# Heads of six tiles side by side with lagging low parts; norm sums and factors within a seventh tile

## What is computed

```python
def rms_norm(x, g):
    y = x * lax.rsqrt(jnp.mean(x * x, axis=-1, keepdims=True) + EPS)
    return y * g

xn = rms_norm(h, g_mix_pre);  z = xn @ w_in;  ...
h = h + rms_norm(mix, g_mix_post)
ff = jnp.square(jax.nn.relu(rms_norm(h, g_mlp_pre) @ w_up)) @ w_down
h = h + rms_norm(ff, g_mlp_post)
gate = jax.nn.sigmoid(rms_norm(h, g_ple_pre) @ w_ple_gate)
h = h + rms_norm((p @ w_ple_proj) * gate, g_ple_post)
# second block
z = rmsnorm(x, ln_mix_g) @ w_in_2;  ...;  x = x + merged @ w_out_2
a, u = split(rmsnorm(x, ln_ffn_g) @ w_ffn_in_2)
x = x + (silu(causal_dwconv(a, conv_w, conv_b)) * u) @ w_ffn_out_2
```

## Time and profile before

| | us |
|---|---|
| median of 3 executions (1488.62 to 1489.58) | 1488.74 |
| the profiled execution, its own time | 1483.36 |
| its span (first to last instruction) | 1481.6 |
| PE busy | 1454.1 (98%) |
| DVE busy | 798.1 (54%) |
| ACT busy | 560.2 (38%) |
| POOL busy | 267.8 (18%) |
| mean granted TensorE clock | 0.993 |

### The profile page before, as it was taken

One profiled execution on the slowest core, in us unless ns is written; L12 is line 12 of the kernel. 1 busy time (PEld: TensorE's weight loads), 2 busy tenths in 40 slices (PEclk: granted clock), 3 DMA queues, 4 the chain that ended last, 5 costly groups with the idle time before them and its releaser, 6 DMA issues.

```text
span 1481.6 us, 17750 instructions
## 1 busy us (share of the span) xinstructions
PE 1454.1 (98%) x6978; PEld 1187.9 (80%) x6978; DVE 798.1 (54%) x1155; ACT 560.2 (38%) x829; POOL 267.8 (18%) x180
## 2 busy tenths in 40 slices
PE   9999999999999999999999999999999999999998
PEld 7876768888888887767888888888887888888887
DVE  5687365433333346675767734634435665534554
ACT  5354434522324224443455546322224443323310
POOL 4255344300101012441033201300003000000000
PEclk9999999999999999999999999999999999999999
DMA  6221222332333332221211211323332233332331
GB/s 229 86 71 58 59 70 86 114 100 87 105 94 100 100 91 81 71 71 58 86 43 44 65 50 57 100 85 100 100 100 85 72 114 100 99 100 86 103 100 69
DMA packets 36131, 129.18 MB, mean 87 GB/s; under 512 B 4024, under 2 KB 4280, under 8 KB 36048
## 3 DMA queue, kind: packets, MB, share of 16 engines
q1 hardware_dynamic: 35760, 127.78, 27.8%
q10 hardware_dynamic: 288, 0.26, 0.1%
HBM read 125.91 MB, written 2.10 MB: 86 GB/s over the span
## 4 chain that ended last, share of the span: by engine, by line
PE 88%; DVE 5%; ACT 3%; issue 2%; POOL 2%; DMA 0%; ACTq 0%; DVEq 0%; POOLq 0%
PE P L1082 26%; PE P L1084 26%; PE P L1083 26%; PE P L1341 1%; POOL AC L2353 1%; PE P L1227 1%; DVE P L1895 1%; POOL H L2362 1%; DVE WST L2108 1%; PE P L1123 1%; PE P L1207 1%; PE P L1178 1%; PE P L1303 1%; POOL DD L2353 1%; PE P L1189 0%
## 5 line engine op out<-in xcount | busy, mean ns | idle before, releaser
L1082 PE MATMUL P<-AH,WH 128*128 128x512 f32 x1104 | 443.1, 401 | 10.0 <-issue 4.4
L1084 PE MATMUL P<-AH,WL 128*128 128x512 f32 x1104 | 432.2, 391 | 0.0
L1083 PE MATMUL P<-AL,WH 128*128 128x512 f32 x1104 | 431.9, 391 | 0.0
L1421 ACT ACTIVATE WH<-WR 128x1024 fp32r<-128x1024 f32 x232 | 243.9, 1051 | 339.3 <-PE P L1084 319.4
L1741 DVE TENSOR_TENSOR WL<-WR,WH 128x1024 fp32r<-128x1024 f32 x215 | 278.2, 1295 | 149.5 <-ACT WH L1421 148.9
L1082 PEld LDWEIGHTS P<-AH,WH 128*128 128x128 f32 x1104 | 208.6, 189 | 61.7 <-issue 13.1
L1084 PEld LDWEIGHTS P<-AH,WL 128*128 128x128 f32 x1104 | 208.3, 189 | 44.2
L1083 PEld LDWEIGHTS P<-AL,WH 128*128 128x128 f32 x1104 | 208.6, 189 | 41.9 <-issue 0.7
L1082 PE MATMUL P<-FH,WH 128*128 128x512 f32 x432 | 168.0, 389 | 0.0
L1083 PE MATMUL P<-FL,WH 128*128 128x512 f32 x432 | 168.0, 389 | 0.0
L1084 PE MATMUL P<-FH,WL 128*128 128x512 f32 x432 | 168.0, 389 | 0.0
(11 more groups left out here) (323 smaller groups left out, 1876.5 us busy)
## 6 DMA issues: line engine op xcount, KB each, us to landing
WR<-in_ws SPq DMA_DIRECT2D x232, 512.0 KB, 3.6
out<-Y SPq DMA_DIRECT2D x8, 256.0 KB, 2.0
H<-in_xT SPq DMA_DIRECT2D x3, 512.0 KB, 8.6
C<-in_const SPq DMA_DIRECT2D x1, 946.5 KB, 11.5
H<-in_xT SPq DMA_DIRECT2D x2, 256.0 KB, 4.2
PR<-in_pT SPq DMA_DIRECT2D x1, 512.0 KB, 4.8
WR<-in_ws SPq DMA_DIRECT2D x1, 384.0 KB, 4.7
WR<-in_ws ACTq DMA_DIRECT2D x1, 128.0 KB, 3.7
```

What stands on the lines that cost most here:

```text
L1082: e.matmul(P, wh, xh, start=start, stop=False)
L1083: e.matmul(P, wh, xl, start=False, stop=False)
L1084: ins = e.matmul(P, wl, xh, start=False, stop=stop)
L1421: e.activation(m.WH[:, c % NW, :], m.WR[:, c % NRAW, :], ACT.Copy).then_inc(*at.up("w_hi", "w_hi", c))
```

## The change

- A head has six tiles side by side (all four ring banks, 6 and 7) in every case, then a seventh, `last`, in bank 5, given by a step function `mid(last, j)`: a whole tile (`wide`), or in head 4 the narrow tile of gk (`narrow`, one step per slice now).
- Of the six, slice j runs WH·xh and WL·xh of each tile (`mm_hi`), and then WH·xl of slice j - 1 of each tile (`mm_lo`). The conversions (`ahead`) are named at `mm_hi` for chunks 0 to 2 and at `mm_lo` from chunk 3 on.
- `sums` stands at step 2 of the seventh tile, `spread` at step 6, both in bank 4; `rbc` after the tile.
- The stages' tile lists are moved up by one accordingly: glu(0), up(6), the seventh gate tile, gk, ffn_a(3) are seventh tiles. In the gate stage ple_gated(6) and its square stand before ple_gate(7).
- In mix2 (the last product before head 5) `x_hi`, `x_lo` and `square` of slices 0 to 5 of norm 5 are named within the loop; in head 5 only slices 6 and 7 remain.
- The number of blocks stays 1864.

```diff
+    def narrow(self, name, c0, n, kind):
+        ids = []
+        def step(t, j):
+            if j == 0:
+                ids.append(self.weight(tuple((0, n * q, name, 128 * q, 128, c0, n) for q in range(8))))
+            self.say("mm_narrow", t, ids[0], kind, n, j)
+        return step
+    def wide(self, spec, kind):
+        return lambda t, j: self.block(t, spec[j], (kind, j), j == 0, j == 7)
     def tokens(self, name, c0, nb, kind):
...
             self.say("square", s, 0, 0)
-        else:
+        elif s != "5":
             make(0)
             make(1)
             rest(0)
-        rest(1)
-        make(2)
-        got = [self.ring() for _ in range(3)] + [self.bank(b) for b in (6, 7)[:len(specs) - 4]]
+        if s != "5":
+            rest(1)
+            make(2)
+        got = [self.ring() for _ in range(4)] + [self.bank(6), self.bank(7)]
+        behind = []
+        def low(j):
+            for t, i in zip(got, behind):
+                if i // CH >= 3:
+                    self.ahead(i)
+                self.say("mm_lo", t, i, (x, j), j == 7)
         for j in range(8):
-            if j == 7:
-                self.sums(s, 0)
-            for m, t in enumerate(got):
-                self.block(t, specs[m][j], (x, j), j == 0, j == 7)
+            ids = []
+            for t, spec in zip(got, specs):
+                i = len(self.plan)
+                if i // CH < 3:
+                    self.ahead(i)
+                self.plan.append(spec[j])
+                ids.append(i)
+                self.say("mm_hi", t, i, (x, j), j == 0)
+            if j:
+                low(j - 1)
+            behind = ids
+            if s == "5":
+                if j < 2:
+                    make(j + 6)
+                    rest(j + 6)
+                continue
             if j < 5:
                 make(j + 3)
             if j < 6:
                 rest(j + 2)
-        b = self.spread(s)
-        out = got + [self.tile(specs[len(got)], [(x, j) for j in range(8)])]
+        low(7)
+        last = self.bank(5)
+        for j in range(8):
+            if j == SUMS:
+                self.sums(s, 0)
+            if j == SUMS + 4:
+                b = self.bank(4)
+                self.say("spread", s, b)
+            mid(last, j)
         self.say("rbc", s, b)
-        return out
+        return got + [last]
 
...
         for t in got:
             self.close(t)
         self.onpool = True
-        spec = tuple((0, 4 * j, "w_in", 128 * j, 128, 1280, 4) for j in range(8))
+        step = self.narrow("w_in", 1280, 4, "A1")
         t = self.ring()
-        self.say("mm_narrow", t, self.weight(spec), "A1", 4)
+        for j in range(8):
+            step(t, j)
         self.say("forget_in", t)
         self.close(t)
         self.beside(self.forget())
         for j in range(2):
-            t = self.tile(fm(128 * j), A)
+            t = self.tile(fm(128 * j), A) if j else out[6]
             self.say("glu", j, t)
             self.close(t)
...
-        out = self.head("2", ready, [fu(f) for f in range(6)])
+        out = self.head("2", ready, [fu(f) for f in range(6)], self.wide(fu(6), "A2"))
         self.say("ple_in")
-        for f in range(6):
+        for f in range(7):
             up(f, out[f])
-        for f in range(6, 8):
-            up(f, self.tile(fu(f), A))
+        up(7, self.tile(fu(7), A))
 
...
-        out = self.head("3", ready, [fg(m) for m in range(5)])
+        out = self.head("3", ready, [fg(m) for m in range(6)], self.wide(fg(6), "A3"))
         for m in range(8):
-            t = out[m] if m < 5 else self.tile(fg(m), G)
+            t = out[m] if m < 7 else self.tile(fg(m), G)
+            if m == 7:
+                self.say("ple_gated", 6)
+                self.say("square", "p3", 6, 1)
             self.say("ple_gate", m, t)
             self.close(t)
             if 0 < m < 7:
                 self.say("ple_gated", m - 1)
                 self.say("square", "p3", m - 1, 1)
-        for m in (6, 7):
-            self.say("ple_gated", m)
-            self.say("square", "p3", m, 1)
+        self.say("ple_gated", 7)
+        self.say("square", "p3", 7, 1)
         return self.post("p3", 1)
 
     def mixer2(self, ready):
...
-        out = self.head("4", ready, [fq(j) for j in range(4)] + [fm(at("ka")), fm(at("va"))])
+        out = self.head("4", ready, [fq(j) for j in range(4)] + [fm(at("ka")), fm(at("va"))],
+                        self.narrow(name, at("gk"), 16, "A4"))
         for j in range(5):
             self.say("qk2", j, out[j])
             self.close(out[j])
-        spec = tuple((0, 16 * j, name, 128 * j, 128, at("gk"), 16) for j in range(8))
-        t = self.ring()
-        self.say("mm_narrow", t, self.weight(spec), "A4", 16)
-        self.say("gk_low", t)
-        self.close(t)
         self.say("va_in", out[5])
         self.close(out[5])
+        self.say("gk_low", out[6])
         self.ya = self.yb = 0
...
             t = self.tile([block("w_out_2", 128 * q, 128 * m) for q in range(8)], [("M2", q) for q in range(8)])
             self.say("mix2", m, t)
             self.close(t)
+            if 0 < m < 7:
+                self.say("x_hi", "5", m - 1)
+                self.say("x_lo", "5", m - 1)
+                self.say("square", "5", m - 1, 0)
         return lambda m: None
...
-        out = self.head("5", ready, [fa(0), fa(1), fu(0), fu(1), fa(2), fu(2)])
+        out = self.head("5", ready, [fa(0), fa(1), fu(0), fu(1), fa(2), fu(2)], self.wide(fa(3), "A5"))
...
         first(2, out[4])
         second(2, out[5])
+        first(3, out[6])
+        second(3, self.tile(fu(3), A))
...
-        pairs(range(3, 8))
+        pairs(range(4, 8))
...
+    def mm_hi(t, i, x, start):
+        c, o = i // CH, (i % CH) * 128
+        P, xh = m.bank[t.bank][:], m.x(*x)[0]
+        part = int(o >= FIRST)
+        w.wait_ge(*(at("w_hi", c) if c else at("w_hi0", part)))
+        w.wait_ge(*at("x_hi", *x))
+        if start:
+            free(t)
+        e.matmul(P, m.WH[:, c % NW, o:o + 128], xh, start=start, stop=False)
+        w.wait_ge(*(at("w_lo", c) if c else at("w_lo0", part)))
+        e.matmul(P, m.WL[:, c % NW, o:o + 128], xh, start=False, stop=False)
+    def mm_lo(t, i, x, stop):
+        c, wh, wl, ends = weights(i)
+        w.wait_ge(*at("x_lo", *x))
+        ins = e.matmul(m.bank[t.bank][:], wh, m.x(*x)[1], start=False, stop=stop)
+        if stop:
+            ins.then_inc(*at.up("full", "full", t.id))
+            if ends:
+                at.also(("full", t.id), "w_used", c)
+        elif ends:
+            ins.then_inc(*at.up("w_used", "w_used", c))
```

More of the change, by code:

```diff
@@ L23 @@
 NBLK = 1864
+SUMS = 2
 NCHUNK = (NBLK + CH - 1) // CH
@@ L292, in spread, with head @@
         return t
-    def head(self, s, ready, specs):
+    def head(self, s, ready, specs, mid):
         x = "A" + s
```

32 lines of the change are left out of this document (17 added, 15 removed).

## The result

The changed kernel takes 1496.38 us (median of seven executions, 1493.28 to 1501.43), the kernel before 1488.74 (seven, 1488.09 to 1491.35): a ratio of 1.0057, interval 1.004 to 1.0073. It is slower by 7.6 us, where 7.5 was forecast. Comparing the two spans therefore exaggerates, and one reading has to come first: the clock.

A forecast was written before the change was run, and what follows sets the result against it. TensorE was taken to bound the kernel, busy 1454.1 of 1481.6 us. The terms gave +5.3 and clock slumps +2.2, total +7.5: 1496.2 us for the median, 0.5% slower; own range 1492 to 1500, full range 1486 to 1502.5.

The forecast's parts named there:

- Part 1: Head starts, needing only x(0)'s high part: heads 2 and 4 win 1.8 us, head 3 0.8, head 5 1.65; head 1 loses 1.1.
- Part 2: Sums and factors within the seventh tile: the waits of 0.66 and 3.28 us before the sums of heads 2 and 3 go.
- Part 3: Evictions after the seventh tile, all ring banks full: head 1 +2.0 us, head 2 0, heads 3 and 5 +0.7 each, head 4 +0.4.
- Part 4: Weight conversions queued behind seven evictions come late: stalls of +2.7 us after head 2 and +4.8 after head 5.
- has 5.5: After head 2's late conversion, the next chunk follows 3.8 us later and has 5.5 us; after head 5 no recurrence either.
- Part 5: Gate tiles of head 3: p3's sums 15.6 us after the seventh tile, some 9 us idle, only -1.5 of 7 won.
- Part 6: Forget gate before the first attention scores: a wait of about 2 us, half absorbed, so +1.0.
- the bound: Forget gate: bounds of 0 and 4 us, as glu(0) and five taps of 0.75 may come in between.
- Clock: Clock slumps behind the new conversion stalls: 1.7 us for head 5 and 0.5 for head 2, together +2.2.
- every stall is paid in full: Rival: slumps of 1.7 us at head 1, forget and head 2, forget wait not absorbed: +13, 1502; chance 0.17.
- Late conversions don't arise: Rival: conversions after heads 2 and 5 reach their queues in time, no stalls or slumps there: 1485 to 1486.5; chance 0.16.
- Gains and losses cancel: Rival: half the conversion stalls, no slump, head 4 at its full gain: +2, 1490.7; chance 0.15.

The follow-up runs named there:

- e3: The changed kernel with the sums at step 0 of the seventh tile instead of 2, factors likewise earlier: span x clock 1473.2 us, 6.0 below the changed kernel.
- e9: The changed kernel with sums and spread at steps 0 and 4, and tiles of up(7), ffn_u(3) and ffn_a(4) named early: median 1.002 of before.
- e1: The changed kernel with the tile of ffn_u(3) named directly behind the first eviction after head 5: span x clock 0.4 us lower than the changed kernel.
- 33 executions: The kernel before, unchanged, run beside the first experiments: median 1486.8 us, mean clock loss 12.9, span x clock 1472.4.
- e4: The kernel before with only norm 5's operands and squares for slices 0 to 5 made inside mix2: ratio 0.999 to before.
- e7: The changed kernel with head 3 and its gate tiles as in the kernel before: span x clock 0.9 us lower than the changed kernel.
- e8: The kernel before with lagging low parts and late sums in heads 2 to 5, five tiles (four in head 3), early norm 5 operands: 1479.24 us, ratio 0.9951.
- e11: The kernel before with late sums in heads 2 to 5 and early norm 5 operands, five tiles (four in head 3), no lag: span x clock 1470.6 us.
- e10: The kernel before with only lagging low parts in heads 2 to 5, sums where they were: 1499.3 us.
- e2: The changed kernel with up(7)'s tile named behind the first eviction after head 2: span x clock 3.0 us lower, clock loss 18.4 us.

## Why the prediction was right

*Starts of heads (Part 1).* Head 2 gained 1.84 (forecast 1.8), head 3 0.83 (0.8), head 5 1.65 (1.65). Head 4's row shrank by 1.25 only, but the gain of 1.8 is there: the first product used to come 1.90 us after the end of AH (644.53) and now comes 0.05 after it (655.56). The idle row starts at the end of the filler matmuls in front, and before, at a reduced clock, four of these took 2.52 us where they now take 1.88, so they hid part of the wait. Chunk 1 in head 1: the tokens come 7.72 later, 5.46 of it the extra tile and 1.16 the wait in front of them, which leaves 1.10 (forecast 1.1; the start of the program alone scatters by some 0.3 between executions).

*Sums within the seventh tile (Part 2).* No wait at either place. The step was right but not looked at from the other side: that the sums stood two steps later than they had to was worth 6.0 us (e3), the largest single term, and the forecast carried it inside Parts 3 to 5 without naming it.

*Evictions (Part 3).* Tokens 1.16 + 0.40 for 1.4 + 0.6; behind head 3 0.31 for 0.7, behind head 4 0.28 for 0.4, behind head 5 0.40 for 0.7. All were somewhat too large.

*Late conversions (Part 4).* The two chains came out as computed: R to conversion 17.44 us (forecast 17.45), copy to end of split 22.55 (22.7), waits 2.50 (2.7) and 4.52 (4.8). e3 and e9 shorten the chains and the waits follow. Only the confidence that the next chunk "has 5.5" us in hand belongs to mlp1; behind head 5 it has none (e1).

*Gates (Part 5).* The sums of p3 stand 15.7 us after the seventh tile's end (629.55), forecast 15.6. The wait in front is 7.11, not 9: between the last gate tile and the sums stand six filler matmuls that the sum left out:

```profile
635.43 2.74 PE L1238 MATMUL P<-C 128*128 128x512 f32 x6
```

They fill time and change nothing, so the elapsed time was right: head 3's start and gates together -1.2, forecast -1.5.

The rows also show who stretches whom beside GpSimd's adds of AC. The weight split took 1.97 us at 640.56, against the 2.03 of the earlier trace rows. The gates' TB steps, with one input in PSUM, kept 0.69; the Y steps, with both inputs in SBUF, grew from 0.69 to 1.06 and, the last one, to 1.25, and five adds of GpSimd took 8.19 (1.64 each, 1.29 alone). That is the pairing that the Trainium skill names (SBUF — State Buffer, "Who interferes with whom"). What it costs is, in the rows, about what GpSimd's instruction still has to run. Two places, of the gates and of the forget chain below:

```profile
643.87 1.26 POOL L2431 TENSOR_TENSOR AC<-AC,SQ 128x512 f32<-128x512 f32 x1 [2.42 <-ACT SQ L1521]
644.43 1.25 DVE L2089 TENSOR_TENSOR Y<-PJ,TB 128x512 f32<-128x512 f32 x1 [0.70 <-ACT TB L1631]
...
73.80 2.40 POOL L2421 TENSOR_TENSOR WL<-WR,WH 128x1024 fp32r<-128x1024 f32 x1 [7.28 <-ACT WH L1499]
73.91 2.83 DVE L1912 SCALAR_TENSOR_TENSOR FX<-FX 4x512 f32<-4x512 f32 x1
```

The add had 0.70 us left and the Y step took 0.56 more than its 0.69; GpSimd's split had 2.29 left and the FX step took 2.15 more than its 0.68. So the 0.8 of the earlier trace rows was right for this split, but it is no bound: a step that begins just behind GpSimd's can wait for nearly the whole of it.

*Forget gate (Part 6).* Mis-sized. The wait is 3.73, forecast about 2. VectorE's timeline:

```profile
68.39 0.67 DVE L1957 TENSOR_TENSOR UP<-P,SG 128x512 f32<-128x512 f32 x1
...
70.87 3.13 DVE L1973 SCALAR_TENSOR_TENSOR P<-UP,PM,P 128x512 f32<-128x512 f32 x4
78.02 0.42 DVE L1917 TENSOR_SCALAR FX<-FX 4x512 f32<-4x512 f32 x1
```

glu(0)'s product and five taps, 4.5 us, now stand between the forget steps; the prediction named them as what might come in between, but left them to the bound. They lengthen the chain by less than they take, from 8.94 us (59.34 to 68.28) to 10.66 (67.78 to 78.44), because VectorE used to be idle for 2.64 of these us. A smaller part of the miss is the transfer: from the last forget step to the first scores were 2.58 us, where some 2 was assumed. (An FX step stretched beside a GpSimd split, 2.83 here, was there before with 2.44.) Part of the wait is absorbed as argued: from the first scores to p1's sums the changed trace is 1.57 us shorter net of the clock, VectorE's 1.07 having gone. Net of both, forget costs about 2.2 us and not 1.

*Clock.* Forecast +2.2; it is +3.8 against the 33 executions and +0.8 against the seven. The argument (a slump behind 4.8 us of idle, none or a third of one behind 2.5) fits the profiled execution in these two places and misses the others:

```profile
81.00:85.00 4.00, 3.98 (x11) 3.23 (x12) 3.23 (x8) 1.82 (x2) 0.00 (x0) 0.50 0.30 114
...
644.00:648.00 4.00, 2.72 (x13) 2.75 (x14) 1.25 (x1) 1.03 (x2) 1.14 (x1) 0.50 0.29 115
...
1188.90:1192.90 4.00, 3.98 (x11) 3.19 (x12) 3.04 (x4) 1.58 (x2) 0.00 (x0) 0.57 0.43 131
```

(stretch, us, busy time of PE, PEld, DVE, ACT and POOL, granted clock, DMA share, GB/s). The falls behind the 3.73 and the 7.11 were not in the sum, though Part 5 had forecast 9 us of idle there, and three more (at 164, 708 and 928 us) have no wait over 0.6 us in front.

*The sum.* The parts were added up in elapsed time, and head 3's -1.5 counts the slumps behind 2.13 and 3.28 us as gone, 3.4 us of clock loss in the windows of before. So the 5.3 is no forecast of the rest, and the 2.2 is not the whole clock: taken apart, the forecast was about +8.7 and -1.2, and the means over the executions gave +6.8 and +3.8. In the two profiled executions, net of the clock, by the stretches above:

```
place                          forecast   measured, net of the clock
head 1 with the forget gate      +4.1       +4.6
head 2                           +0.2       +0.1
head 3 with its gates            -1.5       +0.9   (-1.2 elapsed)
head 4                           -1.4       -1.3
head 5                           +3.9       +3.2
sum                              +5.3       +7.5
```

The mechanism came out as forecast at every place, and the terms within 0.7 us, head 3's in elapsed time. That the total is right to 0.1 us is luck: a clock that cost more than forecast makes up for waits that cost less, and the seven executions of before took more than its 33 later ones.

Of the rivals, *every stall is paid in full* was closer than its 0.17: the forget wait was nearly of its size, a slump did follow it, and the 9.5 us against the 33 executions lie between the forecast and its 13. *Late conversions don't arise* failed at the very place that it named: from the copy to the end of the split were 22.55 us behind head 5, and 17.9 would have been in time. (*Gains and losses cancel* was added up wrongly: 5.3 less half of the conversion stalls, 3.75, and less 0.4 are 1.2 and not 2.)

## What to carry to other kernels

When work is moved off the start of a stage, look at what stands behind the stage in the queues of the engines that evict: a conversion for a chunk three ahead is late by as much as the evictions before it, and one tile more costs both its own eviction and the delay of the factor that all of them need. Count the chain from the factor to the conversion against the blocks until its chunk, as in Part 4; its waits held to 0.3 us here. And two edits that each seem to help (a lagging low part, later sums) can need each other: the lag alone (with the conversions that move with it) cost 0.8%, with late sums it is part of the fastest version (0.5% faster than before), and that version has no seventh tile.

## What the hardware showed that was not expected

The clock falls at places where TensorE doesn't wait, and in one execution but not in another. In mixer 2 eight matmuls whose operands fill 16 of the 128 partitions (PT, GKU) take 3.70 us, 0.45 from start to start where the others take 0.2275. Windows around them, columns as above, of the changed kernel:

```profile
704.00:708.00 4.00, 4.00 (x11) 1.76 (x10) 2.93 (x4) 1.23 (x2) 0.00 (x0) 0.95 0.00 0
708.00:712.00 4.00, 4.00 (x15) 3.53 (x14) 3.50 (x3) 0.58 (x1) 0.00 (x0) 0.50 0.00 0
```

and of the kernel before, at the same instructions:

```profile
696.00:700.00 4.00, 4.00 (x11) 1.78 (x10) 2.92 (x4) 1.25 (x2) 0.00 (x0) 1.00 0.00 0
700.00:704.00 4.00, 4.00 (x25) 3.45 (x23) 3.51 (x3) 2.21 (x3) 0.00 (x0) 1.00 0.02 4
```

Eleven matmuls in 4 us both times; once the clock then fell to its lower level (0.50, which is 1.2 GHz), once it stayed at 2.4 GHz. Of the fourteen profiled executions here the clock fell at this place in eleven; it stayed in before, e4 and e7. Each such fall costs about 1.7 us. The kernel before carries 11 to 14 us of them on average and the changed kernel 16.7; the means over 6 to 12 executions are lowest where few long waits are left (8.5 for e8, 11.2 for e4 and e11, though before itself had 11.1 beside e4) and highest where waits of 5 to 6 us stand in the heads (18.7 for e10). But e1 lost 12.9 and e2 18.4 with nearly the same rows of idle, so what decides a single fall stays open. A gain of 1 to 3 us is visible in the rest, span x clock, before it is visible in the time.
